# A two-layer mixture-of-experts block: norms by token part, the last stores by token part, and an aligned expert loop

## The chip, the cores and the metric

One core of a Trainium2 chip runs the whole program. The metric is the device time of one execution in microseconds (us). The kernel before took 996.31 us, the median of three runs (993.85 to 996.83).

## What is computed

256 latent tokens of width 1024 (and 256 context tokens that only feed the first mixer) pass two layers. Each layer has a mixer and then a grouped mixture of experts, each behind an RMS norm whose result is scaled and shifted by rows computed from a conditioning vector. Cut to what matters here:

```python
for i in range(2):
    mod = split(silu(c) @ ada_w[i] + ada_b[i], 6)        # six rows of 1024
    h   = rmsnorm(x, norm_mix_g[i]) * (1 + mod[1]) + mod[0]
    o   = even_mixer(h, ...) if i == 0 else fourier_mix(h, w_fnet)   # both end in a 1024x1024 product
    x   = x + mod[2] * o
    f   = rmsnorm(x, norm_ffn_g[i]) * (1 + mod[4]) + mod[3]
    y   = grouped_moe(f, ...)      # 1 of 4 groups, top 2 of its 4 experts, 16 experts of 3 x 1024x512
    x   = x + mod[5] * y
return rmsnorm(x, final_g)
```

All of it is float32.

## The kernel before, in words

Every engine has its own instruction list, written by hand, and the engines wait for one another through counting semaphores. An engine works its list strictly in order, so whatever stands behind a waiting instruction waits as well. The 256 latent tokens are two parts of 128 (`TT` = 2), one token a partition; `xl` holds them, `f_` the normed rows.

**The last product of a mixer** (lines 1609 and 1797) makes four 128x512 results in banks 0 to 3: q = 0 to 3, with column half q // 2 and token part q % 2. Part 0 is thus complete after q = 2 and part 1 after q = 3. VectorE adds each to `xl` (`residual`, line 1129; two operations each, lines 1136 and 1137, semaphore `mix_used`). In layer 0 VectorE still has the late modulation sums (`ada0`, line 879) ahead of that in its list.

**The norm behind it.** ScalarE squares each part with a sum (`norm2`, line 738; semaphore `sq_ready`), VectorE turns both sums into means (line 938, `ms_ready`), ScalarE takes both roots (line 747, `root_ready`), VectorE the reciprocals (line 943) and then, a part at a time, a multiplication (line 1161) and a shift add (line 1167), each followed by `h_ready`. In `by_k` norms, those ahead of the experts, both write `f_` by columns with a stride of 128 elements. Between residual and norm stands `prepare` (line 1170), with memsets and four copies of the output gate, and inside the norm the scaled gain (line 1149), one operation over 1024 columns.

**Experts.** TensorE (`experts`, line 1620) begins with `keep_busy(14, 7)`, 14 matmuls whose result nobody reads, then per part eight 128x128 transposes (line 1630) with `keep_busy(2, 7)` between the parts, the router (lines 1636 and 1641) and the ranks (1650). VectorE routes (`route`), GpSimd (POOL) scatters the rows to memory in four indirect DMAs (line 553), and units of 32 tokens then run through gate and up (line 1694), the turned product (1681) and down (1707). TensorE's loop over the experts 1 to 15 is `pe.Fori(0, ROUNDS)` at line 1749, five rounds of three experts each; an expert with more than 32 tokens runs further units in an inner loop.

**Weight loads.** SyncE (SP) issues loads of 1 MB each, six per expert, three experts being held. In layer 1 the loads at line 475 into four of the slots wait for the end of the last product, the next ones for the router product (`part_ps`) and for `h_ready`, and those of expert 3 and later for an expert to have begun.

**Between the layers.** ScalarE copies modulation rows that TensorE sums over partitions (`sum_mod1`, line 1766; copies at line 825): eight ahead of the norm of layer 1's mixer and four behind it. TensorE's tenth and later sum wait for earlier copies; then two keep-warm matmuls, then the DFT (line 1783), which waits for `h_ready` 8.

**The end.** The final norm has no shift; one DMA stores both parts (line 527) and SP waits for it.

Of the kernel before, what the change touches and what calls it, by code (L numbers as in the profile page):

```python
# [19 lines left out]
ALU = mybir.AluOpType  # L20
# [3 lines left out]
P = 128  # L24
D = 1024
# [139 lines left out]
def program(nc, x, ctx, cvec, adaw, adab, gmix, gffn, w_in, w_out, convw, gateb, lamv, subln, fnet, rw, rb,  # L165
            wg, wu, wd, gfin, consts, scratch, out):
    es = ExitStack()
    with es:
# [103 lines left out]
        JUNK = KD * W + 4 * D  # L272
        assert JUNK + TT * D <= KD * W + 6 * D and 4 * HW_ <= 8 * D
# [149 lines left out]
        def _(sp):  # L423
# [102 lines left out]
            sp.wait_ge(h_ready, H_FIN)  # L526
            sp.dma_start(out.rearrange("(t p) d -> p t d", p=P), f_).then_inc(stored, 16)
            sp.wait_ge(stored, 16)
# [63 lines left out]
        def _(act):  # L592
# [145 lines left out]
            def norm2(k, x_wait):  # L738

                if k != 3:  # L740
                    root_table(k)
                for t in range(TT):
                    x_wait(t)
                    nc.scalar.activation(arena[:, JUNK + t * D:JUNK + (t + 1) * D], xl[:, t, :], ACT.Square,
                                         accum_out=ssq[:, t:t + 1]).then_inc(sq_ready, 1)
                act.wait_ge(ms_ready, k + 2)
                nc.scalar.activation(rstd[:, 0:TT], rstd[:, 2:2 + TT], ACT.Sqrt).then_inc(root_ready, 1)
# [101 lines left out]
        def _(dve):  # L849
# [86 lines left out]
            def mean_root(n, i, between=None):  # L936
                dve.wait_ge(sq_ready, 2 * n + 2)
                nc.vector.tensor_scalar(rstd[:, 2:4], ssq[:, 0:2], 1.0 / D, EPS, ALU.mult, ALU.add
                                        ).then_inc(ms_ready, 1)
                if between:  # L940
                    between()
                dve.wait_ge(root_ready, i)
                link(nc.vector.reciprocal(rstd[:, 4:6], rstd[:, 0:2]))

# [184 lines left out]
            def residual(n, banks, gate):  # L1129

                for q, b in enumerate(banks):
                    hf, t = q // 2, q % 2
                    dve.wait_ge(mix_ps, n + q + 1)
                    sl = slice(hf * W, (hf + 1) * W)
                    tmp = sgt[:, q % 2, :]
                    link(nc.vector.tensor_tensor(tmp, ps[b][:], gate[:, sl], ALU.mult))
                    nc.vector.tensor_tensor(xl[:, t, sl], xl[:, t, sl], tmp, ALU.add).then_inc(mix_used, 1)
                dve.wait_ge(mix_used, n + len(banks))
# [3 lines left out]
            def norm_mod(n, i, scale, shift, wait_gain, mods_ready=0, by_k=False):  # L1142

                def scaled_gain():
                    if mods_ready:
                        dve.wait_ge(mod_ready, mods_ready)
                    dve.wait_ge(*wait_gain)
                    if scale is not None:
                        nc.vector.scalar_tensor_tensor(scale, scale, 1.0, gain[:], ALU.add, ALU.mult
                                                       ).then_inc(gain_used, 1)  # L1150

                mean_root(n, i, scaled_gain)
                if scale is not None:
                    dve.wait_ge(gain_used, n)
                g = gain[:] if scale is None else scale
                def cols(a):
                    return a.rearrange("p (m k) -> p m k", k=KD) if by_k else a

                for t in range(TT):
                    dst = f_kd[t] if by_k else f_[:, t, :]  # L1160
                    ins = nc.vector.scalar_tensor_tensor(dst, cols(xl[:, t, :]), rstd[:, 4 + t:5 + t], cols(g),
                                                         ALU.mult, ALU.mult)
                    if mods_ready:
                        dve.wait_ge(mod_ready, mods_ready + 2)
                    if shift is not None:
                        link(ins)
                        ins = nc.vector.tensor_tensor(dst, dst, cols(shift), ALU.add)
                    ins.then_inc(h_ready, 1)

            def prepare(l, gate):  # L1170

                nc.vector.memset(ys, 0.0).then_inc(L[l]["y_ready"], 1)
                nc.vector.memset(runA, 0.0)
                nc.vector.memset(runB, 0.0)
                for j in range(JN):
                    ins = nc.vector.tensor_copy(gate_s[j * S:(j + 1) * S, :], gate[j * S:(j + 1) * S,
                                                                                   j * XW:(j + 1) * XW])
                link(ins)
# [173 lines left out]
            residual(0, [0, 1, 2, 3], mod0[:, 0, :])  # L1352
            dve.wait_ge(mod_ready, 8)
            prepare(0, mod0[:, 3, :])
            norm_mod(2, 4, mod0[:, 2, :], mod0[:, 1, :], (gain_in, 32), by_k=True)
# [3 lines left out]
            norm_mod(3, 5, mod1[1], mod1[0], (gain_late, 16), 8 + 2)  # L1359
# [8 lines left out]
            residual(4, [0, 1, 2, 3], mod1[2])  # L1368
            prepare(1, mod1[5])
            norm_mod(4, 6, mod1[4], mod1[3], (gain_late, 32), by_k=True)  # L1370
# [479 lines left out]
```

## Time and profile before

| | |
|---|---|
| median of three runs | 996.31 us (993.85 to 996.83) |
| the profiled execution | 998.04 us, of which the span is 996.2 us |
| TensorE matmuls busy | 824.4 us (83% of the span) |
| VectorE busy | 390.6 us (39%) |
| ScalarE busy | 179.4 us (18%) |
| moved by DMA | 320.54 MB, mean 322 GB/s |
| mean granted TensorE clock | 0.896 |

The profiler's names: PE is a matmul on TensorE, PEld a weight load there, DVE VectorE, ACT ScalarE, POOL GpSimd, SP SyncE; SPq and ACTq are the DMA issues of those queues. A float32 matmul of 512 columns shows as two records. Times in rows are us from the start of the span; "x28" counts records; in brackets stands the engine's idle time before and what ended it. PEclk and the granted clock are shares of full speed.

### The profile page before, as it was taken

The page shows a single profiled execution, that of the slowest core. Times are in us where ns is not written, and L with a number is a line of the kernel's source. Part 1 is how long each engine was busy: PE and PEld are TensorE (multiplying, and loading weights), DVE is VectorE, ACT ScalarE, POOL GpSimd, SP SyncE. Part 2 cuts the span into 40 slices and gives each one's busy share as a digit, 9 for nine tenths or more (in the row PEclk, how much of TensorE's full clock was granted, in tenths as well). Part 3 has the DMA queues.
Part 4 walks back from the last instruction along what each step waited for, and adds up shares of the span by engine and source line. Part 5 has one row for each costly group of instructions (what it writes and reads, how often), then busy time and mean ns, then how long its engine had stood idle before and what let it go on. Part 6 is the DMA issues. An engine that isn't in the chain of part 4 may idle for free.

```text
span 996.2 us, 18127 instructions
## 1 busy us (share of the span) xinstructions
PE 824.4 (83%) x6940; PEld 441.4 (44%) x6941; DVE 390.6 (39%) x882; ACT 179.4 (18%) x385; POOL 37.9 (4%) x63
## 2 busy tenths in 40 slices
PE   8899899988989968986659976899869879697590
PEld 3544646444554434543325532374435445254240
DVE  3267879858978742111102210423611111121113
ACT  3221010316430201111101110421111111111101
POOL 0000000120001010000000000100010000000001
PEclk9699989998979988998779987899979989798795
DMA  9899877999307888689999899892779999999943
GB/s 339 289 351 352 321 255 275 358 358 310 130 1 257 343 350 331 248 317 414 418 415 417 324 415 351 297 379 90 293 296 411 371 414 416 415 417 413 417 167 134
DMA packets 102841, 320.54 MB, mean 322 GB/s; under 512 B 12944, under 2 KB 28176, under 8 KB 86288
## 3 DMA queue, kind: packets, MB, share of 16 engines
q1 hardware_dynamic: 78432, 282.84, 72.5%
q0 software_dynamic: 4592, 21.41, 5.8%
q10 hardware_dynamic: 19776, 15.75, 4.9%
q8 instruction: 25, 0.41, 0.2%
q14 instruction: 16, 0.13, 0.0%
HBM read 303.58 MB, written 24.64 MB: 329 GB/s over the span
## 4 chain that ended last, share of the span: by engine, by line
PE 33%; issue 28%; DMA 13%; SPq 11%; DVE 9%; ACT 2%; ACTq 1%; POOL 1%; DVEq 0%; POOLq 0%
PE bank L1472 7%; SPq L475 6%; DMA raw<-in_w_up 5%; DMA arena<-unit_rows 4%; PE bank L1408 4%; PE bank L1694 4%; PE bank L1614 3%; PE bank L1803 3%; SPq L444 3%; DMA ring<-in_w_in 2%; PE bank L1476 2%; PE bank L1707 2%; PE bank L1481 1%; SPq L460 1%; DVE arena L879 1%
## 5 line engine op out<-in xcount | busy, mean ns | idle before, releaser
L1694 PE MATMUL bank<-raw,arena 128*32 128x256 f32 x3392 | 250.3, 437 | 73.0 <-DMA raw<-in_w_up 44.3
L1694 PEld LDWEIGHTS bank<-raw,arena 128*32 128x32 f32 x3392 | 119.7, 122 | 183.3 <-DMA raw<-in_w_up 61.1
L1290 DVE TENSOR_TENSOR arena<-arena,bank 64x256 f32<-64x256 f32 x53 | 22.5, 424 | 358.9 <-ACT arena L788 358.9
L1707 PE MATMUL bank<-raw,arena 128*32 128x256 f32 x1696 | 110.5, 387 | 0.8 <-DVE arena L1278 0.8
L1707 PEld LDWEIGHTS bank<-raw,arena 128*32 128x32 f32 x1696 | 59.4, 113 | 40.0 <-issue 3.8
L1472 PE MATMUL bank<-ring,arena 128*128 128x512 f32 x160 | 70.0, 594 | 0.3 <-DMA ring<-in_w_in 0.3
L879 DVE SCALAR_TENSOR_TENSOR bias<-ring,small,bias 128x512 f32<-128x512 f32 x84 | 63.2, 752 | 3.0
L1681 PE MATMUL bank<-consts_sb,arena 64*128 64x64 f32 x212 | 36.0, 292 | 33.9 <-DVE arena L1290 29.9
L788 ACT ACTIVATE arena<-bank 64x256 f32<-64x256 f32 x53 | 19.9, 376 | 238.1 <-PE bank L1694 208.6
L1408 PE MATMUL bank<-consts_sb 128*128 128x512 f32 x132 | 61.9, 616 | 0.0
L1681 PEld LDWEIGHTS bank<-consts_sb,arena 64*128 64x128 f32 x212 | 28.5, 193 | 43.9 <-DVE arena L1290 33.7
L1472 PEld LDWEIGHTS bank<-ring,arena 128*128 128x128 f32 x160 | 30.1, 190 | 38.4 <-issue 37.2
L791 ACT COPY arena<-arena 128x256 f32<-128x256 f32 x53 | 21.4, 404 | 120.7 <-DMA arena<-unit_rows 79.6
L879 DVE SCALAR_TENSOR_TENSOR arena<-ring,small,arena 128x512 f32<-128x512 f32 x56 | 42.1, 752 | 2.0
L788 ACT ACT_TABLE_LOAD x16 | 20.5, 1283 | 105.4 <-issue 105.4
L1285 DVE TENSOR_TENSOR arena<-bank,arena 128x256 f32<-128x256 f32 x53 | 22.5, 424 | 38.6 <-PE bank L1707 38.0
L1408 PEld LDWEIGHTS bank<-consts_sb 128*128 128x128 f32 x132 | 25.2, 198 | 28.0 <-issue 28.0
L1462 PE MATMUL bank<-arena,ring 128*128 128x512 f32 x64 | 30.6, 640 | 1.4 <-DVE arena L931 1.4
L1476 PE MATMUL bank<-arena,ring 128*128 128x512 f32 x64 | 29.8, 626 | 0.0
L1614 PE MATMUL bank<-ring,arena 128*128 128x512 f32 x64 | 28.0, 595 | 0.8 <-ACT arena L731 0.8
L1803 PE MATMUL bank<-ring,arena 128*128 128x512 f32 x64 | 27.6, 592 | 0.0
L561 POOL DMA_INDIRECT arena<-unit_results,row_i x8 | 7.6, 951 | 512.7 <-ACT small L818 510.8
(238 smaller groups left out, 815.5 us busy)
## 6 DMA issues: line engine op xcount, KB each, us to landing
raw<-in_w_gate SPq DMA_DIRECT2D x64, 1024.0 KB, 19.2
raw<-in_w_up SPq DMA_DIRECT2D x64, 1024.0 KB, 21.0
raw<-in_w_down SPq DMA_DIRECT2D x64, 1024.0 KB, 22.2
ring<-in_ada_w SPq DMA_DIRECT2D x24, 2048.0 KB, 13.1
ring<-in_w_in SPq DMA_DIRECT2D x7, 2048.0 KB, 14.3
unit_results<-arena ACTq DMA_DIRECT2D x244, 32.0 KB, 7.2
arena<-unit_rows ACTq DMA_DIRECT2D x55, 128.0 KB, 6.9
ring<-in_w_out SPq DMA_DIRECT2D x2, 2048.0 KB, 41.5
```

Of the source, the lines that this page charges most:

```text
L475: sp.dma_start(dst, src).then_inc(full[s], 16)
L788: nc.scalar.activation(sg[64:P, :], ps[4][0:64, 0:FW], ACT.Silu).then_inc(E["silu_done"], 1)
L879: ins = nc.vector.scalar_tensor_tensor(acc, w[:, k, :], cc[:, k:k + 1], first if k == 0 else acc, ALU.mult, ALU.add)
L1408: mm(ps[bank][:], ident, K_[:, CONSTS["le"][0]:CONSTS["le"][0] + W], start=True, stop=True)
L1462: ins = mm(bank[:], w[:, k, 256 * b + par:256 * (b + 1):2], hT[:, k, :], start=(k == 0), stop=(k == KD - 1))
L1472: ins = mm(bank[:], hT[:, k, t * P:(t + 1) * P], w[:, k, :], start=(k == 0), stop=(k == KD - 1))
L1476: ins = mm(bank[:], w[:, k, a * HD:(a + 1) * HD], hT[:, k, :], start=(k == 0), stop=(k == KD - 1))
L1614: ins = mm(ps[q][:], mgT[:, k, t * P:(t + 1) * P], slot(s)[:, k, :], start=(k == 0), stop=(k == KD - 1))
L1681: ins = mm(ps[6][:, q * 64:(q + 1) * 64], he[64:P, q * P:(q + 1) * P], ident[64:P, 64:P], start=True, stop=True)
L1694: ins = mm(ps[4][o:o + S, 0:FW], xT[:, i, j * S:(j + 1) * S], w[:, k % 4, h * FW:(h + 1) * FW], start=(k == 0), stop=(k == KD - 1))
L1707: ins = mm(ps[5][j * S:(j + 1) * S, 0:XW], hT_e[:, k % QN, k // QN * S:(k // QN + 1) * S], w[:, k % 2, j * XW:(j + 1) * XW], start=(k == 0 ...
L1803: ins = mm(ps[q][:], FT[:, k, t * P:(t + 1) * P], slot(FNET_AT + hf)[:, k, :], start=(k == 0), stop=(k == KD - 1))
```

## The change

In words:

- The Squares write to a scratch at the start of the arena (`squares`, columns 0 to 2047) and no longer into the place of `fT`.
- ScalarE, per token part: Square, wait for that part's mean, root. VectorE, per part: mean, reciprocal, multiplication, shift add (`norm`). In `by_k` norms the multiplication writes contiguously into `squares` and only the shift add writes `f_` by columns.
- `mix_in` replaces `residual`, `prepare` and `norm_mod`: memsets of `runA` and `runB`, the gate copies and the scaled gain come ahead of the residual, then residual q = 0 to 2, norm of part 0, residual q = 3, norm of part 1, and the memset of `ys` at the very end.
- The norm between the layers waits for four more modulation rows at its start (`mod_ready` 12), and its scaled gain stands ahead of the mean. The final norm goes by parts as well.
- The final store is two DMAs of one part each, each waiting for its part.
- TensorE: `keep_busy(14, 7)` is gone, and `keep_busy(2, 7)` between the two parts' transposes becomes `keep_busy(5, 7)`.
- TensorE's expert loop is loaded so that its first instruction is the first one of a fetch block of the code (`head_slot` 0); it may be entered by a branch over padding.

```diff
@@ SyncE
-            sp.wait_ge(h_ready, H_FIN)
-            sp.dma_start(out.rearrange("(t p) d -> p t d", p=P), f_).then_inc(stored, 16)
-            sp.wait_ge(stored, 16)
+            for t in range(TT):
+                sp.wait_ge(h_ready, H_FIN - TT + t + 1)
+                sp.dma_start(out[t * P:(t + 1) * P, :], f_[:, t, :]).then_inc(stored, 16)
+            sp.wait_ge(stored, 16 * TT)
@@ ScalarE, norm2
                 for t in range(TT):
                     x_wait(t)
-                    nc.scalar.activation(arena[:, JUNK + t * D:JUNK + (t + 1) * D], xl[:, t, :], ACT.Square,
+                    nc.scalar.activation(squares[:, t, :], xl[:, t, :], ACT.Square,
                                          accum_out=ssq[:, t:t + 1]).then_inc(sq_ready, 1)
-                act.wait_ge(ms_ready, k + 2)
-                nc.scalar.activation(rstd[:, 0:TT], rstd[:, 2:2 + TT], ACT.Sqrt).then_inc(root_ready, 1)
+                    act.wait_ge(ms_ready, 3 + 2 * (k - 2) + t + 1)
+                    nc.scalar.activation(rstd[:, t:t + 1], rstd[:, 2 + t:3 + t], ACT.Sqrt).then_inc(root_ready, 1)
@@ VectorE
+            def scaled_gain(n, scale, wait_gain):
+
+                dve.wait_ge(*wait_gain)
+                nc.vector.scalar_tensor_tensor(scale, scale, 1.0, gain[:], ALU.add, ALU.mult).then_inc(gain_used, 1)
+                dve.wait_ge(gain_used, n)
+
+            def norm(n, t, g, shift, by_k=False):
+
+                at = 2 * (n - 2) + t
+                dve.wait_ge(sq_ready, NT + at + 1)
+                nc.vector.tensor_scalar(rstd[:, 2 + t:3 + t], ssq[:, t:t + 1], 1.0 / D, EPS, ALU.mult, ALU.add
+                                        ).then_inc(ms_ready, 1)
+                dve.wait_ge(root_ready, 3 + at + 1)
+                link(nc.vector.reciprocal(rstd[:, 4 + t:5 + t], rstd[:, t:t + 1]))
+                even = squares[:, t, :] if by_k else f_[:, t, :]
+                ins = nc.vector.scalar_tensor_tensor(even, xl[:, t, :], rstd[:, 4 + t:5 + t], g, ALU.mult, ALU.mult)
+                if shift is not None:
+                    link(ins)
+                    if by_k:
+                        ins = nc.vector.tensor_tensor(f_kd[t], even.rearrange("p (m k) -> p m k", k=KD),
+                                                      shift.rearrange("p (m k) -> p m k", k=KD), ALU.add)
+                    else:
+                        ins = nc.vector.tensor_tensor(even, even, shift, ALU.add)
+                ins.then_inc(h_ready, 1)
+
+            def mix_in(l, gate, scale, shift, out_gate, wait_gain):
+
+                n = 2 + 2 * l
                 nc.vector.memset(runA, 0.0)
                 nc.vector.memset(runB, 0.0)
                 for j in range(JN):
-                    ins = nc.vector.tensor_copy(gate_s[j * S:(j + 1) * S, :], gate[j * S:(j + 1) * S,
-                                                                                   j * XW:(j + 1) * XW])
-                link(ins)
+                    nc.vector.tensor_copy(gate_s[j * S:(j + 1) * S, :], out_gate[j * S:(j + 1) * S,
+                                                                                 j * XW:(j + 1) * XW])
+                scaled_gain(n, scale, wait_gain)
+                for q in range(3):
+                    residual(4 * l, q, gate)
+                dve.wait_ge(mix_used, 4 * l + 3)
+                norm(n, 0, scale, shift, True)
+                residual(4 * l, 3, gate)
+                dve.wait_ge(mix_used, 4 * l + 4)
+                norm(n, 1, scale, shift, True)
+                nc.vector.memset(ys, 0.0).then_inc(L[l]["y_ready"], 1)
...
-            norm_mod(3, 5, mod1[1], mod1[0], (gain_late, 16), 8 + 2)
+            dve.wait_ge(mod_ready, 8 + 4)
+            scaled_gain(3, mod1[1], (gain_late, 16))
+            for t in range(TT):
+                norm(3, t, mod1[1], mod1[0])
...
-            norm_mod(5, 7, None, None, (gain_late, 48))
+            dve.wait_ge(gain_late, 48)
+            for t in range(TT):
+                norm(5, t, gain[:], None)
@@ TensorE, experts
-                keep_busy(14, 7)
                 for t in range(TT):
                     if t:
-                        keep_busy(2, 7)
+                        keep_busy(5, 7)
                     pe.wait_ge(h_ready, 2 * (2 + 2 * l) + t + 1)
...
-                with pe.Fori(0, ROUNDS) as r:
+                with nc.Fori(0, ROUNDS, engines=bass.OrderedEngineSet([pe.engine]), head_slot={pe.engine: 0}) as r:
```

## Rows read from the trace of the kernel before

**Rows 1.** The page's slices: the span in 40 equal parts, moved GB/s in each.

```profile
GB/s 339 289 351 352 321 255 275 358 358 310 130 1 257 343 350 331 248 317 414 418 415 417 324 415 351 297 379 90 293 296 411 371 414 416 415 417 413 417 167 134
```

**Rows 2.** Chain of waits in order of time: start us, length us, what.

```profile
329.12 12.21 PE bank L1408 x28
...
690.24 12.02 PE bank L1408 x28
```

**Rows 3.** Timeline, layer 1's last product and norm: start us, us, engine, instruction [idle].

```profile
683.41 0.69 DVE L1136 TENSOR_TENSOR arena<-bank,arena 128x512 f32<-128x512 f32 x1 [5.45 <-PE bank L1803]
...
690.27 0.69 DVE L1136 TENSOR_TENSOR arena<-bank,arena 128x512 f32<-128x512 f32 x1 [5.45 <-PE bank L1803]
...
695.47 2.00 DVE L1161 SCALAR_TENSOR_TENSOR arena<-xl,small,arena 128x1024 f32<-128x1024 f32 x1
...
697.50 1.94 DVE L1167 TENSOR_TENSOR arena<-arena 128x1024 f32<-128x1024 f32 x1
...
701.37 1.97 DVE L1167 TENSOR_TENSOR arena<-arena 128x1024 f32<-128x1024 f32 x1
...
704.68 1.04 PE L1630 MATMUL bank<-consts_sb,arena 128*128 128x128 f32 x8
```

**Rows 4.** Timeline, the same place in layer 0.

```profile
325.03 0.69 DVE L1136 TENSOR_TENSOR arena<-bank,arena 128x512 f32<-128x512 f32 x1
...
328.41 0.69 DVE L1137 TENSOR_TENSOR xl<-xl,arena 128x512 f32<-128x512 f32 x1
...
331.90 0.89 DVE L1176 COPY arena<-arena 32x256 f32<-32x256 f32 x3
...
340.13 1.96 DVE L1167 TENSOR_TENSOR arena<-arena 128x1024 f32<-128x1024 f32 x1
...
343.76 1.04 PE L1630 MATMUL bank<-consts_sb,arena 128*128 128x128 f32 x8
```

**Rows 5.** TensorE in the experts (timeline), then stretches: busy times, PEclk, DMA share, GB/s.

```profile
736.18 1.11 PE L1681 MATMUL bank<-consts_sb,arena 64*128 64x64 f32 x4 [8.74 <-DVE arena L1290]
737.22 5.57 PE L1694 MATMUL bank<-raw,arena 128*32 128x256 f32 x64
...
745.48 3.66 PE L1694 MATMUL bank<-raw,arena 128*32 128x256 f32 x64
...
433.00:437.00 4.00, 0.19 (x2) 0.00 (x0) 0.71 (x2) 0.41 (x1) 0.00 (x0) 1.00 1.03 425
...
702.00:706.00 4.00, 3.72 (x21) 2.38 (x19) 1.34 (x1) 1.75 (x4) 0.00 (x0) 1.00 0.03 13
...
727.00:736.00 9.00, 0.44 (x6) 0.20 (x2) 0.30 (x1) 1.96 (x3) 0.00 (x0) 0.72 0.67 269
```

**Rows 6.** Timeline between the layers.

```profile
636.39 2.61 DVE L1346 SCALAR_TENSOR_TENSOR xl<-arena,xl 128x1024 f32<-128x1024 f32 x2 [1.25 <-DMA arena<-unit_results,row_i]
...
640.30 1.22 DVE L1149 SCALAR_TENSOR_TENSOR arena<-arena,gain 128x1024 f32<-128x1024 f32 x1
...
642.96 0.59 ACT L825 COPY arena<-bank 128x512 f32<-128x512 f32 x1 [2.34 <-PE bank L1766]
...
645.48 1.88 PE L1408 MATMUL bank<-consts_sb 128*128 128x512 f32 x4
...
645.55 1.23 DVE L1167 TENSOR_TENSOR arena<-arena 128x1024 f32<-128x1024 f32 x1
```

**Rows 7.** Timeline of the end, then the final store: KB, us from issue to landing.

```profile
987.38 1.06 ACT L744 ACTIVATE arena<-xl 128x1024 f32<-128x1024 f32 x1 [1.76 <-DVE xl L1346]
...
988.34 0.19 ACT L744 ACTIVATION_READ_ACCUMULATOR arena<-xl 128x1 f32 x1
...
989.27 2.48 DVE L1161 SCALAR_TENSOR_TENSOR arena<-xl,small,gain 128x1024 f32<-128x1024 f32 x2
...
out<-arena SPq DMA_DIRECT2D x1, 1024.0 KB, 4.0
```

**Rows 8.** Chain of waits, where layer 0's expert loop turns back for the first time.

```profile
433.19 3.99 issue
```

More of the change, by code:

```diff
@@ L271, in program @@
         Z, C = fo["Z"], fo["C"]
-        JUNK = KD * W + 4 * D
-        assert JUNK + TT * D <= KD * W + 6 * D and 4 * HW_ <= 8 * D
+        squares = arena[:, 0:TT * D].rearrange("p (t n) -> p t n", t=TT)
+        assert 4 * HW_ <= 8 * D
         FT = lay([("FT", (KD, SEQ))], 2048)[0]["FT"]
@@ L934, in _ @@
             nc.vector.memset(lam_s[:, 6:7], 0.0).then_inc(gain_used, 1)
[L936 to L943, printed above, removed]
             dve.wait_ge(smalls_in, 16 * 7)
@@ L1127, in _ @@
                 ada0(c)
[L1129 to L1138, printed above, removed]
@@ L1140, in _ @@
-            sgt = arena[:, 6144:6144 + 1024].rearrange("p (a n) -> p a n", a=2)
[L1142 to L1165, printed above, removed]
-                        link(ins)
-                        ins = nc.vector.tensor_tensor(dst, dst, cols(shift), ALU.add)
-                    ins.then_inc(h_ready, 1)
@@ L1170, in prepare, with residual @@
-            def prepare(l, gate):
-                nc.vector.memset(ys, 0.0).then_inc(L[l]["y_ready"], 1)
+            def residual(n, q, gate):
+                hf, t = q // 2, q % 2
+                dve.wait_ge(mix_ps, n + q + 1)
+                sl = slice(hf * W, (hf + 1) * W)
+                tmp = sgt[:, q % 2, :]
+                link(nc.vector.tensor_tensor(tmp, ps[q][:], gate[:, sl], ALU.mult))
+                nc.vector.tensor_tensor(xl[:, t, sl], xl[:, t, sl], tmp, ALU.add).then_inc(mix_used, 1)
@@ L1175, in prepare @@
                 for j in range(JN):
-                    ins = nc.vector.tensor_copy(gate_s[j * S:(j + 1) * S, :], gate[j * S:(j + 1) * S,
-                                                                                   j * XW:(j + 1) * XW])
-                link(ins)
+                    nc.vector.tensor_copy(gate_s[j * S:(j + 1) * S, :], out_gate[j * S:(j + 1) * S,
[9 more added lines that the diff above has]
+                nc.vector.memset(ys, 0.0).then_inc(L[l]["y_ready"], 1)
             def route(l):
@@ L1350, in combine_results @@
                     ins.then_inc(added, 1)
-            residual(0, [0, 1, 2, 3], mod0[:, 0, :])
             dve.wait_ge(mod_ready, 8)
-            prepare(0, mod0[:, 3, :])
-            norm_mod(2, 4, mod0[:, 2, :], mod0[:, 1, :], (gain_in, 32), by_k=True)
+            mix_in(0, mod0[:, 0, :], mod0[:, 2, :], mod0[:, 1, :], mod0[:, 3, :], (gain_in, 32))
             route(0)
@@ L1367, in _ @@
             dve.wait_ge(mod_ready, 8 + N_ADA)
-            residual(4, [0, 1, 2, 3], mod1[2])
-            prepare(1, mod1[5])
-            norm_mod(4, 6, mod1[4], mod1[3], (gain_late, 32), by_k=True)
+            mix_in(1, mod1[2], mod1[4], mod1[3], mod1[5], (gain_late, 32))
             route(1)
```

## The prediction

> **What bounds the kernel now.** I read the views from coarse to fine. The slices of the page first: the moved bytes sit at 410 to 418 GB/s through most of both expert stages and fall to 90 GB/s around 672 to 697 us and stay below 300 up to 747 us [rows 1]. So the expert stages are limited by the weight stream, and the stretch ahead of them, where the last product, the norm and the routing follow one another, is limited by a chain of small steps in which the DMA engines go idle. Next the chain of waits: in both layers it runs through 28 records of line 1408 (14 keep-warm matmuls) for 12.02 to 12.21 us directly behind the product [rows 2]. That says TensorE's filling matmuls, not only the norm, hold the transposes back. The timelines then show what is late if they go.
>
> Layer 1: the product ends at 690.24 [rows 2]; the last residual part starts at 690.27, the first norm write at 695.47 and the last shift add ends at 701.37 + 1.97 = 703.34; the second transposes start at 704.68, 1.3 us later, behind the second helping of keep-warm matmuls [rows 3]. Layer 0: VectorE is late itself, because its last modulation sums end at 325.03, when three of the four products are already there; its last shift add ends at 340.13 + 1.96 = 342.09, and the second transposes start at 343.76 [rows 4].
>
> **Prices used.** A residual quarter is two operations of 0.69 us, 1.41 us with the wait between them (0.03 us, as between the writes at 695.47 and 697.50 [rows 3]); three in a row took 328.41 + 0.69 - 325.03 = 4.07 us [rows 4]. A Square with its accumulator read takes 988.34 + 0.19 - 987.38 = 1.15 us [rows 7]. Mean, root and reciprocal take 989.27 - (988.34 + 0.19) = 0.74 us [rows 7]. A by-column write costs 2.00 us in the multiplication and 1.94 us in the addition [rows 3]; the same multiplication into contiguous memory costs 2.48 / 2 = 1.24 us alone [rows 7], and four contiguous operations with their waits took 645.55 + 1.23 - (640.30 + 1.22) = 5.26 us, 1.3 each [rows 6]. The changed kernel writes the product contiguously and only the sum by columns: 1.3 + 1.94 + 0.1 for the wait, about 3.3 us a part instead of 3.9. If the strided write isn't what costs the addition its time, 2.6 us; if the mixed form is no cheaper, 3.9; I take 3.3, the row of the strided multiplication (contiguous in, strided out) being the nearest. Keep-warm: 12.02 / 28 = 0.43 us a record, two a matmul, so keep_busy(5) is 4.3 us.
>
> **Layer 1.** Gate copies, small memsets and the scaled gain (three copies in 0.89 us [rows 4] and one more, 1.2 us; 1.22 us [rows 6]) go ahead of the product, where VectorE waits some six microseconds for each quarter: nothing, as long as the gain has landed (POOL asks for it about 20 us before). Part 0: its second half is quarter 2, at 683.41, done 684.82; Square to 686.01, root chain to 686.75, 3.3 us more: ready at 690.1, when the product ends. So the first transposes follow the product at once, to 691.2, and keep_busy(5) ends at 695.5. Part 1: quarter 3 from 690.27 to 691.68, Square to 692.9, chain to 693.6, writes to 697.0. The second transposes start at 697.0 instead of 704.68: **-7.7 us**. The ys memset (0.91 us) moves behind it, where VectorE waits about 4 us for the affinities: nothing. Bounds for this term: -8.4 (the addition at the contiguous price) to -5.0 (TensorE cools in the 1.5 us gap and its transposes, router and logit matmuls, 2.7 us in all, run at half speed).
>
> Does this shift reach the end? The loads into slots 12 to 17 wait for the router product, and the DMA engines are idle ahead of it (share 0.03 between 702 and 706) and 0.67 busy between 727 and 736 [rows 5], while all later loads wait for an expert begun. Nothing between 690 and 738 is tied to an absolute time except four loads that are issued at the product's end, and these finish about 702. Pulled forward, ten loads of 1 MB follow one another from 690.3; at 2.5 us each they end at about 717, while the row scatter then begins near 713. Before, it was about the same overlap. I pass the shift on in full and give 1 us of the range to this contention.
>
> **Layer 0.** VectorE is the late one, and the copies and scaled gain now lie on its path ahead of the first residual: 1.2 + 1.22 = 2.4 us, to 327.45. Three quarters to 331.55, Square (VectorE idles: quarter 3 is queued behind this wait) to 332.74, chain to 333.5, writes to 336.8. Quarter 3 to 338.2, Square to 339.35, chain to 340.1, writes to 343.4: 1.3 us later than 342.09. The keep-warm matmuls are gone, so TensorE idles from 329.1 to 336.9 and then has transposes 1.04 and keep_busy(5) 4.3, to 342.2 at full clock. After an idle time of 8.74 us the same 64 records took 5.57 instead of 3.66 us [rows 5], 1.9 us lost; with that, 344.1. So the second transposes start at 344.1 against 343.76: **+0.4 us**. Bounds: 343.5 (warm, -0.3) and 347.5 (all at half clock, +3.8). The 14 removed matmuls thus buy nothing in layer 0: the norm takes their place as the late one.
>
> **Between the layers.** ScalarE now waits for the mean of part 0 before it squares part 1, and the modulation copies 8 to 11 are queued behind the second root. VectorE: combine ends at 636.39 + 2.61 = 639.00; the scaled gain, hidden behind the second Square before, now lies open (1.22 us [rows 6]); chain 0.7, two contiguous operations 2.6, second chain, two more: ready at 646.8, as before (645.55 + 1.23 = 646.78). But the copies, which began at 642.96, now follow the second root at about 643.9, and the eleventh and twelfth column sums on TensorE wait for them: two sums of two 0.43 us records, then four keep-warm records of 1.9 us, to 648.0 instead of 645.48 + 1.88 = 647.36 [rows 6]: **+0.7 us**. Bounds 0 to +1.5.
>
> **The end.** Combine ends at 987.35, just ahead of the second Square at 987.38 [rows 7]. Now mean of part 0 at once, chain 0.74 to 988.1, write 1.2; Square of part 1 meanwhile; mean at 989.3, chain to 990.0, write to 991.25, store asked at 991.3 instead of 991.78 (989.27 + 2.48 [rows 7]). One store of 1 MB took 4.0 us from issue to landing [rows 7]; at the stream's 415 GB/s [rows 1] 2.5 us of these are bytes. Part 0's half is asked for near 989.3 and out of the way; half the bytes save 1.3: **-1.8 us** in all. Bounds -0.5 (the landing takes 4.0 us whatever the size) to -2.3.
>
> The Trainium skill speaks against this split: "SBUF — State Buffer", section "The DMA setup-cost knee", says each transfer pays roughly 2 us whatever its size and advises the largest single transfer. With its figure for each of two halves in series the end would come at about 995.7 (estimate from that page) and the split would bring next to nothing. The row shows a fixed share of 4.0 less 2.5, 1.5 us, and nothing on whether two of them overlap; rival (d) is the case in which they don't.
>
> **The aligned loop.** TensorE's loop body starts at a block boundary of the code, entered by one jump. The entry falls into the 8.7 us in which TensorE waits before the second expert: covered. The trace shows one stall where a loop turns back, 3.99 us ahead of line 1681 at 433.19 in layer 0 [rows 8], and none in layer 1. Would its removal help? The DMA engines are fully busy in it (share 1.03 [rows 5]) and the experts behind wait for weights, so the load backlog covers it. With that cover gone the stall would be on the path, and removing it bring -4.0; code that now arrives late at the same turn in layer 1 costs up to +4.0. I take **0**: the row of the busy DMA engines is the one that bears on this turn.
>
> **Sum.** -7.7 + 0.4 + 0.7 - 1.8 + 0 = -8.4 us. The profiled execution took 998.04 (span 996.2 and 1.8 around it), so 989.6; it lay 1.7 above the median of the three runs, so 996.31 - 8.4 = 987.9, forecast 988.0.
>
> **Rivals.**
> (a) *Cold TensorE.* Without the 14 warm matmuls, the half clock holds through transposes, keep_busy(5) and router in both layers: layer 0 +3.4 on top, layer 1 +2.7: -2.3, 994.0. For: the 1.9 us lost after 8.7 us idle [rows 5]. Against: in layer 1 the product itself runs up to the transposes.
> (b) *A code stall on the path.* The turn of the loop costs 4.0 us in layer 1 too, where no backlog covers it: -4.4, 991.9.
> (c) *Slower.* Aligned, the body and what is fetched behind it no longer stay together, and every turn fetches its head again: four turns a layer, 4.0 us each [rows 8], 32 us in all; those in the weight-bound stretches are covered, half of them as an estimate: +16 - 8.4 = +7.6, 1003.9. It decides from three open stalls upward (12 us against 8.4). Against: in the trace before only the first turn stalls. The Trainium skill, "Runtime: NRT & Kernel Launch", section "Instruction fetch mechanics", says that a taken branch to a target outside the window has to fetch it; this trace's 3.99 us agrees for one turn, and no other turn shows it.
> (d) *Stores in series.* Each half pays 1.5 us of its own and 1.3 us of bytes [rows 7]: 989.3 + 2.8 + 2.8 = 994.9 against 991.78 + 4.0 = 995.8, so the end gives 0.9 and not 1.8 us: 988.8, inside the range. The page named above is for it; one queue serves both stores, and nothing in the trace shows two stores behind one another.
>
> **Chances.** Forecast 0.58; (d) 0.15; (a) 0.12; (b) 0.09; (c) 0.06. The terms' bounds, taken as independent (root of the sum of squares), come to 1.2 us down and 4.6 up without the loop's; a loop gain of 4.0 is less likely than its absence. The range 984.5 to 993.0 holds the forecast, (b) and (d), and leaves out (a), (c) and tails. About 0.3% (3 us) is what a measurement can tell from no change: faster needs less than 993.3: 0.80; same (993.3 to 999.3) 0.14; slower 0.06.
>
> **What the profile after would show.** Layer 1: transposes of line 1630's part 0 directly behind the product, part 1 about 7 us behind its end (14.4 before). Layer 0: first transposes about 8 us behind the product, then keep-warm records longer than 0.43 us. Between the layers: modulation copies bunched behind the second root, the first DFT matmul some 0.7 us later relative to the combine. End: two stores, the last landing under 3 us after its issue. Loop: stalls put down to issue where it turns. The forecast is wrong if the first expert of layer 1 begins less than 6 us nearer to the product's end, or if the shift is there and the DMA share shows new gaps behind it.

## The result and the profile after

The changed kernel took 989.86 us (median of 10 executions) against 996.38 us for the kernel before; the ratio is 0.9925 with a 95% interval of 0.9906 to 0.9943, so 7.5 us faster (5.7 to 9.4). One of the 10 executions ran at a lower granted clock (0.792, 1035.16 us) and is left out of the ratio; the two medians themselves lie 6.5 us apart. The forecast was 8.4 us faster, 988.0 us, in a range of 984.5 to 993.0. The profiled execution took 987.21 us with a span of 985.4 us, 10.8 us below that of before. Not all of it is the change: 3.9 us of the difference are there already at the end of layer 0's modulation sums, in code that is the same in both (325.12 and 321.19 us). Times are therefore compared from one event to the next.

How the two profiles differ, cut at events of the timelines (us; each row is the distance between two events; a unit is the work on 32 tokens of one expert, and its start is that of its turned product):

```
stretch                                                        before   after   change
start -> end of layer 0's modulation sums (same code)          325.12  321.19   -3.93
-> layer 0's second transposes (part 1)                         18.64   19.18   +0.54
-> TensorE starts the second unit (line 1681, now 1676)         31.56   31.53   -0.03
-> last down product of layer 0                                241.64  240.56   -1.08
-> combine done                                                 22.04   21.82   -0.22
-> first DFT matmul                                              8.20    8.77   +0.57
-> end of layer 1's last mixer product                          43.04   43.03   -0.01
-> layer 1's second transposes (part 1)                         14.44    6.65   -7.79
-> TensorE starts the second unit                               31.50   33.04   +1.54
-> last down product of layer 1                                234.92  236.34   +1.42
-> combine done                                                 16.25   16.57   +0.32
-> end of the span                                               8.85    6.72   -2.13
sum                                                            996.20  985.40  -10.80
```

Layer 1 in the timeline of the changed kernel (start us, length us, engine, line, instruction, in brackets the idle time before it and what ended it); it answers [rows 3]:

```profile
679.25 0.69 DVE L1127 TENSOR_TENSOR arena<-bank,arena 128x512 f32<-128x512 f32 x1 [5.45 <-PE bank L1798]
...
683.90 1.93 DVE L1151 TENSOR_TENSOR arena<-arena 128x1024 f32<-128x1024 f32 x1
...
685.92 1.06 PE L1625 MATMUL bank<-consts_sb,arena 128*128 128x128 f32 x8
...
686.82 4.46 PE L1404 MATMUL bank<-consts_sb 128*128 128x512 f32 x10
...
690.77 1.90 DVE L1151 TENSOR_TENSOR arena<-arena 128x1024 f32<-128x1024 f32 x1
...
692.73 1.09 PE L1625 MATMUL bank<-consts_sb,arena 128*128 128x128 f32 x8 [1.45 <-DVE arena L1151]
```

Part 0's norm is ready at 685.83, when the product ends at 686.08, and its transposes follow without a gap. The last shift add ends at 692.67 and the second transposes start at 692.73: they now wait for the norm and no longer for keep-warm matmuls. Layer 0 is different; it answers [rows 4]:

```profile
331.00 1.91 DVE L1151 TENSOR_TENSOR arena<-arena 128x1024 f32<-128x1024 f32 x1
...
332.96 1.97 PE L1625 MATMUL bank<-consts_sb,arena 128*128 128x128 f32 x8 [7.67 <-DVE arena L1151]
...
334.72 5.81 PE L1404 MATMUL bank<-consts_sb 128*128 128x512 f32 x10
...
337.38 1.93 DVE L1151 TENSOR_TENSOR arena<-arena 128x1024 f32<-128x1024 f32 x1
...
340.37 1.04 PE L1625 MATMUL bank<-consts_sb,arena 128*128 128x128 f32 x8
```

TensorE idles 7.67 us, then the same eight transposes take 1.97 instead of 1.04 us and the ten keep-warm records 5.81 instead of 4.46 us. The norm is done at 339.31; the transposes start 1.06 us later, behind the keep-warm matmuls. A stretch of the same place (its start and end, its length, the busy times of PE, PEld, DVE, ACT and POOL, then PEclk, DMA share, GB/s) shows the level of the clock: 0.50, which is 1.2 of 2.4 GHz.

```profile
329.00:337.00 8.00, 4.04 (x11) 2.78 (x12) 5.98 (x9) 2.52 (x6) 0.00 (x0) 0.50 1.01 417
```

Between the layers and at the end, which answer [rows 6, 7] (the last row: DMA issue, KB each, us from issue to landing):

```profile
637.48 1.88 PE L1761 MATMUL bank<-arena,consts_sb 128*128 128x512 f32 x4
...
639.54 1.96 PE L1761 MATMUL bank<-arena,consts_sb 128*128 128x512 f32 x4 [0.18 <-ACT arena L826]
...
643.05 7.31 PE L1778 MATMUL bank<-consts_sb,arena 128*128 128x129 f32 x64
...
981.03 1.28 DVE L1147 SCALAR_TENSOR_TENSOR arena<-xl,small,gain 128x1024 f32<-128x1024 f32 x1
...
out<-arena SPq DMA_DIRECT2D x2, 512.0 KB, 2.6
```

What had not been forecast stands in two other places. First, the row scatter of layer 1: from the fourth scatter issue to the first row load that waits for it 10.0 us instead of 8.5 us.

```profile
712.41 0.95 POOL L554 DMA_INDIRECT unit_rows<-arena,row_i  x1 [0.30 <-issue]
...
722.41 0.37 ACTq L767 DMA_DIRECT2D arena<-unit_rows  x1
```

Second, gaps in the expert loops that the trace puts down to issue (TensorE waits there for nothing that the profile shows), the first at layer 0's first turn, which answers [rows 8], and one in the third unit of layer 1, which had none in the kernel before:

```profile
434.28 1.10 PE L1676 MATMUL bank<-consts_sb,arena 64*128 64x64 f32 x4 [4.61 <-issue]
...
738.48 1.71 PE L1689 MATMUL bank<-raw,arena 128*32 128x256 f32 x27 [1.45 <-issue]
```

### The profile page after: what moved, and what is told of

Read it like the earlier page. It is cut to its first block, busy times and chain, and to the rows that moved or that the text cites. A ratio compares the mean times of both kernels' runs of the same rounds, so it can differ in the third digit from the quotient of the medians.

```text
span 985.4 us, 18052 instructions
## 1 busy us (share of the span) xinstructions
PE 801.9 (81%) x6896; PEld 430.2 (44%) x6897; DVE 389.2 (40%) x890; ACT 179.9 (18%) x389; POOL 38.0 (4%) x63
## 4 chain that ended last, share of the span: by engine, by line
PE 30%; issue 29%; DVE 15%; DMA 14%; SPq 6%; ACT 2%; ACTq 1%; POOL 1%; POOLq 0%; DVEq 0%
PE bank L1468 7%; SPq L475 5%; DMA raw<-in_w_up 5%; PE bank L1689 4%; DMA arena<-unit_rows 4%; PE bank L1458 3%; PE bank L1798 3%; PE bank L1472 2%; DMA ring<-in_ada_w 2%; PE bank L1702 2%; DVE bias L880 2%; PE bank L1477 1%; DMA arena<-unit_results,row_i 1%; DVE arena L880 1%; DVE arena L1088 1%
## 5 line engine op out<-in xcount | busy, mean ns | idle before, releaser
L1404 PE MATMUL bank<-consts_sb 128*128 128x512 f32 x88 | 44.2, 647 | 0.0
L1273 DVE COPY arena<-bank 128x128 f32<-128x128 f32 x53 | 15.5, 292 | 29.7 <-PE bank L1676 21.7
```

The lines of the kernel that those rows point to most:

```text
L1404: mm(ps[bank][:], ident, K_[:, CONSTS["le"][0]:CONSTS["le"][0] + W], start=True, stop=True)
```

## The experiments

Each starts from the changed kernel (ratio 0.9925) or the kernel before; ratios are to the kernel before. Besides the whole time, whose intervals are about 2 to 4 us to either side, the stretches of the table above are used.

**The keep-warm matmuls and the norm, each alone.**

```diff
 # e3_warm_back: the changed kernel
+                keep_busy(14, 7)
                 for t in range(TT):
                     if t:
-                        keep_busy(5, 7)
+                        keep_busy(2, 7)
 # e4_warm_only: the kernel before
-                keep_busy(14, 7)
                 for t in range(TT):
                     if t:
-                        keep_busy(2, 7)
+                        keep_busy(5, 7)
```

> The changed kernel with the 14 and 2 keep-warm matmuls back ahead of and between the transposes. By my steps the second transposes of layer 1 can start no earlier than 12.0 us (14 keep-warm) + 1.0 + 1.7 behind the product's end, 14.6 us instead of 6.6: the 7.8 us gain of layer 1 is gone, and layer 0 gets within 1 us of the kernel before (second transposes 14.7 us behind the product). Ratio 0.998 to 1.001: the end's 2 us less the 0.6 us between the layers. If the norm by parts carried the gain by itself, the ratio would stay below 0.995.

> The kernel before with only the keep-warm matmuls changed (none ahead, five between). The second transposes then wait for the old norm: ready 13.1 us behind the product in layer 1 instead of a start at 14.4, first transposes near 9.2 behind it with TensorE cold (idle for 9 us), keep-warm 6 us: second transposes at 9.2 + 2 + 5.6 = 16.8, so 2 us later than before, in both layers. Ratio 1.001 to 1.006, slower. If the keep-warm matmuls were the whole cause, ratio 0.993.

Measured: e3 0.9992 (0.9970 to 1.0013), second transposes of layer 1 14.44 us behind the product, and 18.59 us behind the sums in layer 0. With the 14 matmuls back, the norm by parts brings nothing in either layer; only the 2.16 us of the end remain. e4 1.0071 (1.0044 to 1.0099): second transposes 16.55 us behind the product in layer 1 and 20.40 us behind the sums in layer 0, 2.1 and 1.8 us later than before. The timeline of e4 in layer 1 shows why:

```profile
701.76 1.97 PE L1629 MATMUL bank<-consts_sb,arena 128*128 128x128 f32 x8 [9.17 <-DVE arena L1167]
703.52 5.79 PE L1408 MATMUL bank<-consts_sb 128*128 128x512 f32 x10
709.14 1.04 PE L1629 MATMUL bank<-consts_sb,arena 128*128 128x128 f32 x8
```

Idle for 9.17 us, TensorE starts at the low clock, and the keep-warm matmuls hold the transposes back although the norm is done at 705.58. e4's whole time is worse than its two stretches say (7 us against 3.9); about 3 us more stand in its experts of layer 1, with a new gap of 3.0 us there. So neither half of the change gives anything alone in layer 1, and together they give 7.8 us: the second transposes start at the later of two chains that were 1.3 us apart.

**No keep-warm matmuls at all.**

```diff
                 for t in range(TT):
-                    if t:
-                        keep_busy(5, 7)
```

> The changed kernel without the five keep-warm matmuls between the parts' transposes. My step says that in layer 0 they run at half clock and end 1.0 us behind the norm, so without them the second transposes start 1.0 us earlier but at the low clock (2.0 us instead of 1.0), router and logits too: layer 0 even or up to 1.5 us slower. In layer 1 TensorE idles 5.7 us between the transposes: the second ones and the router at half clock, 1 to 3 us slower. If the clock were no matter here, both layers would be 0 to 1 us faster.

Measured: 0.9943 (0.9919 to 0.9967). Layer 0's second transposes come 1.04 us earlier than in the changed kernel, as expected; from there to the fourth scatter it takes 22.57 instead of 20.25 us in layer 0, and 21.69 instead of 19.68 us in layer 1. The stretch with router and ranks in layer 1, first without the five matmuls, then with them:

```profile
700.00:708.00 8.00, 6.83 (x26) 3.27 (x26) 3.03 (x22) 2.64 (x5) 0.00 (x0) 0.50 0.95 357
```

```profile
700.00:708.00 8.00, 5.29 (x20) 2.43 (x18) 6.87 (x37) 0.00 (x0) 0.00 (x0) 1.00 1.01 405
```

The clock falls to 0.50, and from the second transposes on 2.0 us more go by. The second transposes themselves start no later in layer 1 (6.64 us behind the product). The page "TensorE: Matmul & The Clock Gate" of the Trainium skill, section "Why this matters for your kernels", says that idle gaps between bursts of matmuls bring the clock down; these two rows agree. Up to the scatter the five matmuls are thus worth 2.0 us in layer 1 and 1.3 us in layer 0 (2.3 less 1.0). Little of it reaches the experts: the second unit starts 39.98 us behind layer 1's product without them and 39.69 us with them, and 51.55 against 50.71 us behind layer 0's sums, since the later scatter is the faster one (8.0 instead of 10.0 us in layer 1). The whole times (0.9943 and 0.9925) can't tell such a difference.

**The aligned loop.**

```diff
 # e1_no_align: the changed kernel; e2_align_only: the kernel before, the other way round
-                with nc.Fori(0, ROUNDS, engines=bass.OrderedEngineSet([pe.engine]), head_slot={pe.engine: 0}) as r:
+                with pe.Fori(0, ROUNDS) as r:
 # e12_slot_96: the changed kernel
-                with nc.Fori(0, ROUNDS, engines=bass.OrderedEngineSet([pe.engine]), head_slot={pe.engine: 0}) as r:
+                with nc.Fori(0, ROUNDS, engines=bass.OrderedEngineSet([pe.engine]), head_slot={pe.engine: 96}) as r:
```

> The changed kernel with the expert loop laid where the code happens to fall, everything else as changed. If the alignment is worth nothing (my step): ratio to before 0.991 to 0.994 (the changed kernel has 0.9925), span of the experts of layer 1 (first gate product to last down product) within 1 us of the 246.5 us of the changed kernel. If the alignment costs (the 2.9 to 3.5 us waits ahead of the first gate product, put down to issue, belong to it and are not hidden): those waits shrink to about 1 us as before and the kernel gets 1 to 3 us faster. If it saves: the stall at a turn of the loop in layer 1 appears, 4 us, and the kernel is up to 4 us slower.

> The kernel before with the aligned loop alone. No effect: ratio 0.998 to 1.002. If the alignment costs: the wait ahead of the first gate product of each layer grows from 1.0 to about 3 us, and the ratio is 1.001 to 1.004; if it saves, the 4.0 us stall at the first turn of layer 0 goes and the ratio is 0.996 to 0.999.

> The changed kernel with the loop's first instruction on slot 96 of a fetch block instead of 0. If the alignment saves because the position of the loop decides where code arrives late: other stalls than with slot 0 (1.45 us in the third unit of each layer, 4.6 us at layer 0's first turn), among them one of 3 us or more in layer 1's expert loop, and up to 4 us slower. If any fixed position does as well as slot 0: the same stalls within 0.5 us, and experts of layer 1 in 236 to 238 us.

Measured: e1 0.9956 (0.9936 to 0.9976), e2 1.0004 (0.9984 to 1.0023), e12 0.9985 (0.9961 to 1.0009). Experts of layer 1 (second unit to last down product) and the longest gap put down to issue in the loops of the two layers:

```
                                   experts of layer 1   gap in layer 0   gap in layer 1
before (unaligned)                      234.9                4.0              none over 0.8
e2 before, slot 0                       237.9                4.0              1.4
changed, slot 0                         236.3                4.6              1.5
e1 changed, unaligned                   240.2                none over 0.8    3.9
e12 changed, slot 96                    241.9                3.7              3.5
```

The gap of e1 and e12 in layer 1 stands ahead of the turned product of the third unit, which isn't where the loop turns back; first e1, then e12:

```profile
738.84 1.11 PE L1676 MATMUL bank<-consts_sb,arena 64*128 64x64 f32 x4 [3.89 <-issue]
739.88 5.80 PE L1689 MATMUL bank<-raw,arena 128*32 128x256 f32 x64
```

```profile
741.88 1.10 PE L1676 MATMUL bank<-consts_sb,arena 64*128 64x64 f32 x4 [3.54 <-issue]
742.91 6.48 PE L1689 MATMUL bank<-raw,arena 128*32 128x256 f32 x64
```

Only the position of the code differs between these kernels and the changed one. That these gaps are late code can be read from the trace's DMA records. In all 14 profiles each gap over 1 us of the loops that is put down to issue has a block of 16 KB on the instruction queue, inside it or ending within 0.2 us of its start; blocks that move without a gap are there too. Such a block moves from 433.43 to 434.36 in the gap of the kernel before (433.19 to 437.18), from 736.23 to 737.15 in that of e1 (734.95 to 738.84) and from 738.59 to 739.57 in that of e12 (738.34 to 741.88). Ahead of the changed kernel's gap of 1.45 us in layer 1 (737.03 to 738.48) it moves from 736.04 to 737.03. The block itself takes about 1 us; what fills the rest of a gap these records don't show. The place thus decides how much of the wait is open: in layer 1, early in the loop, 3.5 to 3.9 us are lost, and behind it e1 loses 2.6 us more at the low clock (1.11 instead of 0.66 us for the turned product and 5.80 instead of 3.66 us for the 64 records behind it). The changed kernel loses 2.1 us in the same unit, gap included (8.41 us from turned product to turned product against 6.31 for the next). In the other kernels on slot 0 (e2, e3, e5 to e11) the experts of layer 1 took 236.7 to 238.2 us and the gap there was 1.3 to 2.2 us. So the alignment brings the kernel before nothing (its ratio is 1.0004, and in the one pair of profiles the experts of layer 1 even take 3.0 us longer, 1.4 of them the new gap). What it does for the changed kernel is to put a gap of 1.5 us in the place of the 3.9 us that the moved code would otherwise have had. e1 is 3.1 us slower by the ratios, whose intervals overlap at 0.994, and its experts of layer 1 take 3.8 us longer than the changed kernel's and 2.0 to 3.4 us longer than those of the others on slot 0. Slot 96 is a fixed position as well and no better than none.

**The ends of the change.**

```diff
 # e5_one_store
-            for t in range(TT):
-                sp.wait_ge(h_ready, H_FIN - TT + t + 1)
-                sp.dma_start(out[t * P:(t + 1) * P, :], f_[:, t, :]).then_inc(stored, 16)
-            sp.wait_ge(stored, 16 * TT)
+            sp.wait_ge(h_ready, H_FIN)
+            sp.dma_start(out.rearrange("(t p) d -> p t d", p=P), f_).then_inc(stored, 16)
+            sp.wait_ge(stored, 16)
 # e9_between_old: the norm between the layers
+            dve.wait_ge(sq_ready, NT + 4)
+            nc.vector.tensor_scalar(rstd[:, 2:4], ssq[:, 0:2], 1.0 / D, EPS, ALU.mult, ALU.add).then_inc(ms_ready, 2)
             scaled_gain(3, mod1[1], (gain_late, 16))
+            dve.wait_ge(root_ready, 7)
+            link(nc.vector.reciprocal(rstd[:, 4:6], rstd[:, 0:2]))
...
```

> The changed kernel with the one 1 MB store of before. If splitting saves the bytes (my step): from the end of the last multiplication to the end of the span 4.4 us as before, against 3.1 us with two stores; 1.3 us slower than the changed kernel. If two stores pay their fixed share in series (rival d): within 0.4 us of it.

> The changed kernel with the norm between the layers in its old order: both squares, both roots in one, the scaled gain beside them, the late modulation copies right behind. My step gives the new order 0.7 us there: combine to first DFT matmul 8.2 us as before instead of 8.8. If something else delays the DFT, it stays at 8.8. Nothing measurable in the whole time (0.6 us).

Measured: e5 0.9952 (0.9926 to 0.9978); combine to end 8.05 us with one store against 6.72 us with two, 1.33 us, and 8.85 us in the kernel before, so 0.8 us come from the rest, which is the norm by parts. The store of e5 takes as long as before, against 2.6 us for each half above:

```profile
out<-arena SPq DMA_DIRECT2D x1, 1024.0 KB, 4.0
```

e9 0.9921 (0.9889 to 0.9953). Combine to DFT stayed at 8.70 us, so my expectation failed. The timeline says why: this stretch isn't tied to the combine but to TensorE's own list, where eight keep-warm matmuls stand ahead of the late sums. From the first of the late sums to the DFT it is 642.81 - 637.51 = 5.30 us in e9, as in the kernel before (647.20 - 641.90), and 5.57 us in the changed kernel. The order costs 0.27 us, and the rest of the 0.57 us is how the combine happens to lie to TensorE's list (e2, with the old order, has 9.24 us).

**The scatter.**

```diff
                 if s >= MAIN + 2:
                     sp.wait_ge(h_ready, 6 + 4 * l)
+                    if s >= MAIN + 3:
+                        sp.wait_ge(rows_out, 16 * 2 * TT * (l + 1))
```

> The changed kernel with three of the weight loads ahead of the experts (the last three of expert 2) held back until the row scatter has landed. In the changed kernel the first row load is asked for 10.0 us behind the last scatter issue in layer 1, in the kernel before 8.5 us: the scatter shares the DMA engines longer with weight loads. Contention as the cause: with the loads held back that interval falls below 8 us and the experts of layer 1 begin 2 us earlier. If expert 2 then waits for its weights, the gain is given back there (DMA waits of line 1689 near the third unit). If the interval stays at 10 us, it isn't contention with these loads.

Measured: 0.9902 (0.9874 to 0.9931). Fourth scatter to first row load 5.57 us instead of 10.0 us in layer 1, 4.07 instead of 7.68 us in layer 0. The second unit starts 29.34 us behind the second transposes in layer 1 (33.04) and 28.75 us in layer 0 (31.53). Layer 0 gives it back, its experts take 244.1 instead of 240.6 us; layer 1 keeps 2.6 of 3.7 us.

```profile
715.65 0.95 POOL L556 DMA_INDIRECT unit_rows<-arena,row_i  x1 [0.30 <-issue]
...
721.22 0.39 ACTq L769 DMA_DIRECT2D arena<-unit_rows  x1
721.27 0.33 SPq L475 DMA_DIRECT2D raw<-in_w_up  x1
```

So in the changed kernel the scatter is slow because it shares the DMA engines with the weight loads. The kernel before wasn't run with held loads; that a longer overlap made 10.0 us of its 8.5 us is my reading, not shown.

**Layer 0's norm, and a version from all of it.**

```diff
 # e8_prep_early: c == ADA_LATE[-1]; e10_prep_in_wait: c == ADA_LATE[-2]
             for c in ADA_LATE:
+                if c == ADA_LATE[-1]:
+                    dve.wait_ge(mod_ready, 8)
+                    prep(2, mod0[:, 2, :], mod0[:, 3, :], (gain_in, 32)) 
                 ada0(c)
```

> The changed kernel with layer 0's memsets, gate copies and scaled gain ahead of the last late modulation sum, where VectorE waits 1.5 to 2.3 us for a store anyway. My step says that these 2.5 us lie on layer 0's path: residual 2.3 us earlier if they fill the wait, second transposes 1 to 2.3 us earlier, the kernel 1 to 2.3 us faster than the changed one. If layer 0's norm isn't on the path, no change.

> As e8, but ahead of the last but one modulation sum, the one in front of which VectorE waits 2.2 us for the store of a sum. e8 put the same 2.5 us ahead of the last sum, which waits for nothing, and moved nothing. Layer 0's norm being bound by VectorE: measured from the product's end, residual and second transposes come 2 us earlier than in the changed kernel (13.2 us behind the product instead of 15.2), and the kernel is 2 us faster. If the store's wait merely moves behind it, 15.2 again.

> The changed kernel with e10's and e9's orders, and with e7's three held loads in layer 1 only, since layer 0 gave its 2.8 us back to later weight waits. Parts: 2.0 us from e10, 0.6 from e9, 3.7 less 1 from e7 in layer 1: 5 us faster than the changed kernel, ratio to before 0.986 to 0.990. If the parts take one another's place, 0.990 as e7 alone.

Measured from the product's end to layer 0's second transposes: changed 15.20 us, e8 15.63, e10 12.60. e8, 0.9929 (0.9905 to 0.9954), had the operations in the wrong place: the wait is in front of the last but one sum, and ahead of the last one they only delayed it. In e10, 0.9886 (0.9848 to 0.9924), they fill it. e11, with e10, e9 and the held loads in layer 1 only, took 982.76 us, 0.9860 (0.9832 to 0.9887): 14.0 us faster than the kernel before and about 6.5 us faster than the change under study. Its interval lies below those of both kernels.

## Why the prediction was right, point by point

- **Layer 1, -7.7 us: measured -7.8.** Every event lay within 0.3 us of its forecast distance: part 0 ready with the product's end, second transposes 6.65 us behind it (forecast 697.0 - 690.24 = 6.8). The strided addition cost 1.90 to 1.93 us and the contiguous multiplication 1.28 us, as the nearest rows had said. e3 and e4 show that it takes both parts of the change.
- **Layer 0, +0.4 us: measured +0.5.** VectorE's later norm (forecast 1.3 us later; 339.31 against 321.19 is 18.1 us behind the sums, 17.0 before) and a cold TensorE both came as forecast. e10 shows that the copies and the scaled gain on VectorE's path are what layer 0 pays, 2.6 us.
- **That the shift reaches the end: nearly.** The term failed in size: 7.8 us at the transposes were 6.25 at the second unit. I had seen the overlap of scatter and loads and held it for equal; from scatter to row load it cost 1.5 us. My sign of being wrong, the first expert of layer 1 beginning less than 6 us nearer to the product's end, came true as worded: the first gate product begins 27.60 us behind it (713.68 - 686.08) against 33.17 us before (723.41 - 690.24), 5.57 us nearer, because it waits 2.92 instead of 0.96 us. The second unit, the first that needs the scattered rows from memory, is 6.25 us nearer. Over all kernels with the early transposes and no held loads the way from scatter to row load in layer 1 took 9.0 to 10.6 us (e6, whose scatter comes 2 us later, 8.0), with late ones 8.4 to 9.1, so the 1.5 us hold for this pair.
- **Between the layers, +0.7 us: measured +0.57, by another cause in half of it.** The queued copies cost 0.27 us (e9).
- **The end, -1.8 us: measured -2.1.** The split gives 1.3 us (e5), the norm by parts the rest. Rival (d), stores in series, falls: the second store is asked for at about 982.3, before the first has landed (980.53 + 2.6), and the end gave 2.1 us and not 0.9. The page "SBUF — State Buffer" of the Trainium skill, section "The DMA setup-cost knee", says that each transfer pays a fixed share of roughly 2 us. The runs agree that there is one, but a smaller one: 4.0 us for 1 MB and 2.6 us for half of it leave 1.2 us as an estimate. Its advice, one transfer as large as possible, doesn't hold for this last store, whose halves are ready at different times (e5).
- **The aligned loop, 0: measured between 0 and -3 us, and the reason was wrong.** I looked at one gap of 4 us and asked what covers it. It stayed, and stayed covered. What I had not weighed is that the other edits move the code as well: without the alignment the changed kernel stalls 3.9 us in layer 1. Here the number owed something to luck: e1 has every other edit, whose terms come to the same -8.4, and gained 4.4 us (2.4 to 6.4). A stall that no term held and an alignment put at nothing largely cancelled. Rival (b) named the price and the layer, but for the aligned code and at the loop's turn; it came true for the unaligned code, in the third unit. Rival (c), a stall at each turn, fell.
- **Rival (a), cold TensorE through to the router,** is what e6 shows without the five matmuls, 2.3 us in layer 0 and 2.0 us in layer 1 instead of the 3.4 and 2.7 of the rival. With the five matmuls the clock is back ahead of the router: layer 0's second transposes take 1.04 us again.
- **The sum.** The change's own stretches come to -10.80 + 3.93 = -6.9 us in the one pair of profiles, the ratio says -7.5 (5.7 to 9.4), the forecast was -8.4. What the terms did not hold: the way from layer 1's transposes to its second unit +1.5, experts of layer 1 +1.4 (the gap of 1.45 us in the third unit is of that size, but the kernels on slot 0 differ by 1.9 us among themselves), experts of layer 0 -1.1.

What stays open: ahead of the first gate product TensorE waited 0.96 us in the kernel before and 1.6 to 3.6 us in all others, aligned or not. In the changed kernel, e1 and e2 it follows a copy on VectorE in layer 1 that starts 2.6 us late and whose releaser the trace calls remote. In none of the 14 profiles does a block move on the instruction queue in this wait, so it isn't of the kind above. It is hidden behind the row load in every profile, and its cause stays open.

## What to carry to other kernels

When two chains end near the same point, price both: here fillers on TensorE and the norm were 1.3 us apart, and in layer 1 each edit alone was worth nothing or less. Whoever shortens the way to a burst of DMA work should look at what else is in the queues at the new time, and hold back loads that aren't needed soon. After any edit, the gaps put down to issue belong into the comparison, since moved code can open or close a stall of 4 us that has nothing to do with the edit.

## What the runs showed of the hardware

- Position of code alone changed the time by 3 to 6 us: the same instructions with the loop on slot 0, where they fell, and on slot 96 gave ratios of 0.9925, 0.9956 and 0.9985. The blocks of 16 KB on the instruction queue took about 1 us each, and TensorE's gaps around the late ones 3.0 to 5.2 us.
- After 5.3 to 9.2 us of idle time eight 128x128 transposes took 1.97 instead of 1.04 us, at a granted clock of 0.50 (1.2 GHz); after 1.45 us they took 1.09 us.
- Four indirect stores of 128 rows of 4 KB were followed by the row load that waits for them 4.1 to 5.6 us behind the last issue when three loads of 1 MB were kept out of their way, and 7.2 to 10.6 us behind it otherwise.
- Two stores of 512 KB, one behind the other on one queue, landed 2.6 us from issue (the median of the two) against 4.0 us for 1 MB.
